# One modulation piece at a time between dense weight slabs, three bank turns, and moved operands in a two-block transformer kernel

## The chip, the cores and the metric

The kernel runs on one core of a Trainium2 chip, as one program. The metric is the device time of that program in microseconds. Before the change it is 2503.66 us, the median of three runs (2502.77 to 2505.79).

## The reference

Two blocks of two layers each, over 256 tokens of width 1024, all in float32. In short:

```python
def first_block(x, ...):
    for l in range(2):
        h = rms_norm(x, norm_mix_pre[l])
        u = h @ w_in[l]                              # 1024 x 6484
        ys = [mamba2(u), fox(u), moba(u), dsa(u)]    # four branches, 512 wide each
        gates = sigmoid(h @ w_gate[l] + b_gate[l])   # four times 1024
        mix = (sum of gates * (ys @ w_branch[l])) @ w_out[l]
        x = x + rms_norm(mix, norm_mix_post[l])
        h = rms_norm(x, norm_ffn_pre[l])
        g, up = split(h @ w_ffn_in[l], 2)            # 2816 each
        x = x + rms_norm((silu(g) * up) @ w_ffn_out[l], norm_ffn_post[l])

def second_block(x, ctx, c, c_ctx, ...):             # adaLN block on x and on ctx
    for l in range(2):
        # six modulations of width 1024 for the tokens and six for the context
        m = silu(cvec) @ w_mod_2[l] + b_mod_2[l]     # 1024 x 6144
        shift1, scale1, gate1, shift2, scale2, gate2 = split(m, 6)
        h = rms_norm(x) * (1 + scale1) + shift1
        p = h @ w_in_2[l]                            # 2560 columns
        # chunked linear mixing (256), differential attention (4 heads, 512),
        # and a gated convolution of 31 taps (256) side by side
        x = x + gate1 * (y @ w_out_2[l])
        h = rms_norm(x) * (1 + scale2) + shift2
        x = x + gate2 * ((act(h @ w_gate_2[l]) * (h @ w_val_2[l])) @ w_down_2[l])
```

The modulation does not depend on x, so it may be computed at any time before its use. Layer 0 of the second block works on the tokens and on the context (four tiles of 128 rows), layer 1 on the tokens alone (two tiles), and so does the whole first block.

## The kernel before

Every dense product streams its weights. A slab is two blocks of 128 rows by 512 columns (512 KB). SP loads it into one of four ring slots (`wraw`, L898). ScalarE rounds it to the matmul's short format (`whi`, L1009), VectorE makes the rest (`wlo`, L816), and PE multiplies three times for each block and tile: high by high, high by low, low by high (L1770). A slab of two tiles is 12 matmuls of 512 columns, one of four tiles 24. ScalarE and VectorE are three slabs ahead of PE (`AHEAD`). Eight PSUM banks hold the results; the dense products take them in turns of four, the attention and small steps take the other four.

One planner in Python writes a single list of steps, and each engine walks this list in order and does its part of each step. So what stands in the list before something stands before it on every engine. The steps are slabs of the dense products, with the work of the branches woven in between (`weave`, `interleave`).

The modulation product has its own path. Its slabs (`mod_slabs`, 4 slabs for 512 columns, 24 such chunks) aren't split; PE multiplies the raw weights in full precision with the two condition vectors, in four column groups of the array at once. ScalarE copies the sums (`modrow`, L1050), PE adds the groups up and turns them (`mod_cols`) or spreads them over the rows (`mod_gate`), and VectorE adds the bias. The chunks are put at places between two stages (`filler`, `fill`), in the second block's attention (the gates), and between chunks of the second FFN. A ring slot with a modulation slab is free when PE has used it, where that of a dense slab is free as soon as it is split:

```python
if st.s >= RING_W:
    was = slabs[st.s - RING_W]
    need(sp, [was.used if was.evac == "mod" else was.split])
```

In the first block's attention each head's steps are `attn_s` (scores by PE, maximum by VectorE, exponentials by ScalarE, L1228), `attn_t` (PE turns the weights, ScalarE copies them as `probT`, L1232) and `attn_v` (values). In the second block's a unit's steps are `att2_s` (scores, maximum L1465, exponentials L1117), `att2_m` (reciprocal and the difference of two maps, L1472 to L1476), `att2_t` (turn, `aT`, L1123) and `att2_v`. In the stage with gates and branches every third slab's low half is made by POOL. The projections of the second block go to `p`, even tiles by ScalarE, odd ones by VectorE (L1320).

Of the kernel before, what the change touches and what calls it, by code (L numbers as in the profile page):

```python
# [48 lines left out]
RING_W, RING_S, AHEAD = 4, 4, 3  # L49
SLAB_K = 2  # L50
# [8 lines left out]
class Step:  # L59


    def __init__(self, kind, n=None, gain=None, x=None, sums0=None, out0=None, used=None, src=None, col=None,
# [5 lines left out]
                 d=None):  # L68
# [7 lines left out]
        self.ssq0, self.t, self.k0, self.sq, self.n0, self.pool, self.split, self.d = ssq0, t, k0, sq, n0, pool, split, d  # L76


class Planner:
# [6 lines left out]
    def __init__(self):  # L86
        self.steps = []
        self.uses = [0] * 8
        self.count = {}
        self.gemm_banks = 0  # L90
        self.turns = (0, 1, 2, 3)
        self.slabs = []
        self.first_slab, self.x_start = {}, {}
        self.dense = []
        self.mod_chunks = []
# [6 lines left out]
    def misc(self):  # L102

        return self.bank(FREE_BANKS[self.tick("free_turn") % 4])
# [46 lines left out]
def gemm(pl, weight, layer, act, tiles, nk, col0, width, evac, row0=0, kt0=0, ready=(), turned=False, **more):  # L151
# [3 lines left out]
    for c, (a, w) in enumerate(widths(width)):  # L155
# [3 lines left out]
        for k in range(0, nk, SLAB_K):  # L159
# [15 lines left out]
            if evac != "mod":  # L175
                st.d = len(pl.dense)
                pl.dense.append(st)
            steps.append(st)
    return steps


MOD_COLS = (0, 1, 2, 3, 6, 7, 8, 9)
MOD_GATES = (4, 5, 10, 11)


def mod_slabs(pl, l, c):


    n = len(pl.mod_chunks)
    war = pl.mod_chunks[n - 2] if n >= 2 else []  # L190
    pl.mod_chunks.append([])
    return gemm(pl, "w_mod_2", l, "cond", 1, KD, c * NW, NW, "mod", ready=[("cond_silu", 1)], mc=n, war=war)


def mod_reader(pl, slabs, bank):

    st = slabs[-1]
    l, c = st.layer, st.col // NW
    steps = []
    if c in MOD_GATES:  # L200
        banks = [bank(), bank()]
        steps.append(Step(kind="mod_gate", l=l, c=c, mc=st.mc, gate=c // 6, j=c % 2, waits=drained(*st.banks), banks=banks))
    else:
        banks = [bank()]
        steps.append(Step(kind="mod_cols", l=l, c=c, mc=st.mc, waits=drained(*st.banks), banks=banks))
        if c in (3, 9):
            steps.append(Step(kind="mod_gain", l=l, i=c // 6, waits=drained(*banks)))
    pl.mod_chunks[st.mc] += [(f"psum_full{b}", k + 1) for b, k in banks]
    return steps


def plan_first(pl):

    filler = list(MOD_COLS)
    for l in range(DEPTH):
# [32 lines left out]
        if l:  # L248
            pl.steps += mod_reader(pl, mods, pl.misc)
# [9 lines left out]
        def branch_splits(n, waits):  # L259
# [8 lines left out]
               (36, Step(kind="decay_turn", **decay)), (37, cb)]  # L268
        ybanks = [pl.bank(6), pl.bank(7)]
# [13 lines left out]
        def attention(br, qcol, waits):  # L283
# [4 lines left out]
            for i in range(HEADS + 3):  # L288
                for kind, h in (("attn_s", i), ("attn_v", i - 3), ("attn_t", i - 2)):
                    if 0 <= h < HEADS:  # L290
                        q = base + h
                        steps.append(Step(kind=kind, l=l, br=br, h=h, q=q, vcol=qcol + 2 * BW + h * HD,
                                          bank=pl.bank(4 + q % 2 + (0 if kind == "attn_s" else 2)),
# [62 lines left out]
        for st in pl.slabs[first:-len(g)]:  # L356
            st.pool = st.s % 3 == 0
# [3 lines left out]
        if l == 0:  # L361
            pl.add("cond")
# [5 lines left out]
        mods = mod_slabs(pl, 0, filler.pop(0))  # L368
        pl.steps.append(mods[0])
        postnorm(2 * l, out)  # L370
        pl.steps += mods[1:]
# [3 lines left out]
        pl.steps += mod_reader(pl, mods, pl.misc)  # L375
# [18 lines left out]
        mods = mod_slabs(pl, 0, filler.pop(0))  # L394
        pl.steps += mods + waiting + mod_reader(pl, mods, pl.misc)
        out = gemm(pl, "w_ffn_out", l, "hid", 2, KF, 0, D, "mix", ready=split_ready(hidden))
        pl.steps += out
        if l < DEPTH - 1:
            mods = mod_slabs(pl, 0, filler.pop(0))
            pl.steps.append(mods[0])  # L400
            postnorm(2 * l + 1, out)
            pl.steps += mods[1:]
        else:
            postnorm(2 * l + 1, out)


def plan_second(pl):

    filler = [(0, MOD_COLS[-1])] + [(1, c) for c in MOD_COLS]
    for l in range(DEPTH):  # L410
# [3 lines left out]
        def fill():  # L414

            return mod_slabs(pl, *filler.pop(0)) if filler else []

        def norm(i, tiles, summed):

            mods = fill()  # L420
            pl.steps.extend(mods[:1])
# [4 lines left out]
            pl.steps.extend(mods[1:])  # L426
# [5 lines left out]
            if mods:  # L432
                pl.steps += mod_reader(pl, mods, pl.misc)
# [10 lines left out]

        gc = project(C_C, T, ready)
# [31 lines left out]
        pl.steps += weave(gc + gq + gk + ga + gv, others)  # L477

# [7 lines left out]
        for i in range(len(units) + 2):  # L486
            for kind, u in (("att2_m", i - 1), ("att2_t", i - 2), ("att2_s", i), ("att2_v", i - 2)):
# [23 lines left out]
        stream = []  # L511
        agate = Step(kind="agate", l=l, tiles=T, n=aln[0].n, banks=[pl.gemm_bank(), pl.gemm_bank()])
        stream.append(agate)
        late = None
        for i, c in enumerate(MOD_GATES):
            g = mod_slabs(pl, l, c)
            stream += g
            if late:
                stream += mod_reader(pl, late, pl.gemm_bank)
            late = g  # L520
            if i == 1:
                cback = Step(kind="cback", l=l, tiles=T, banks=[pl.gemm_bank() for i in range(T // 2)])
                cln = ln(C_C, 2, drained(*cback.banks))
                cout = Step(kind="csilu", l=l, tiles=T, n=cln[0].n)
                stream += [cback, cln[0]]
            if i == 2:
                stream += [cln[1], cout]
        stream += mod_reader(pl, late, pl.gemm_bank)
# [3 lines left out]
        mods = fill()  # L532
        pl.steps += mods
# [6 lines left out]
        if mods:  # L540
            pl.steps += mod_reader(pl, mods, pl.misc)
# [16 lines left out]
        late = None  # L558
        base = pl.now("hid_lo")
        pl.turns = tuple(range(8))  # L560
        for c, (a, w) in enumerate(widths(FFN)):
            n0 = pl.now("hid_lo")
            for weight, evac in (("w_gate_2", "ffg"), ("w_val_2", "ffv")):
                pl.steps += gemm(pl, weight, l, "act2", T, KD, a, w, evac, ready=ready, turned=True, n0=n0)
                ready = ()
            pl.tick("hid_lo", w // P)
            if late:
                pl.steps += mod_reader(pl, late, pl.misc)
            late = fill() if c in (0, 1, 2, 3) else None
            pl.steps += late or []  # L570
        late = fill()
        pl.steps += late
        if late:
            pl.steps += mod_reader(pl, late, pl.misc)
# [12 lines left out]
def build(nc, A, out, second=True):  # L587
    pl = Planner()
    plan_first(pl)
    if second:  # L590
        plan_second(pl)
    slabs, dense = pl.slabs, pl.dense
# [4 lines left out]
    with ExitStack() as ctx:  # L597
# [44 lines left out]
        stream = sb("stream", [P, 4])  # L642
        cond = sb("cond", [P, KD, 2])
        condm = sb("condm", [P, KD, 32])
        modrow = sb("modrow", [P, 2, NW // 2])
# [4 lines left out]
        modg = sb("modg", [P, DEPTH, 2, KD, 2])  # L650
        psum = ctx.enter_context(nc.psum_tensor("psum", [P, 8, 512], F32))
# [7 lines left out]
        gains = sb("gains", [P, 1, D], F32, one)  # L659
        act_h = sb("act_h", [P, KD, SEQ], F32R, one)  # L660
# [90 lines left out]
        rstd4 = sb("rstd4", [P, 4], F32, two)  # L751
# [4 lines left out]
        p = sb("p", [P, 4, IN_COLS], F32, two)  # L756
        kT = sb("kT", [P, B_HEADS, 4 * P], F32, two)
# [66 lines left out]
        def _(sp):  # L824
# [5 lines left out]
            def load_parameters():  # L830
                o = P
                for t, n, parts in ((tri, P, P), (ones, P, P), (cmask, 3 * P, P), (smask, 3 * P, P), (cossin, 128, P),
                                    (negsel, 16, 16), (cossin2, 128, P), (stream, 4, P)):
# [37 lines left out]
            for st in slabs:  # L871
# [21 lines left out]
                if st.s >= RING_W:  # L893
                    was = slabs[st.s - RING_W]
                    need(sp, [was.used if was.evac == "mod" else was.split])
                w = A[st.weight]
# [1196 lines left out]
```

## Time and profile before

| | |
|---|---|
| median of 3 runs | 2503.66 us (2502.77 to 2505.79) |
| the profiled execution's own time | 2500.43 us |
| its span, first to last instruction | 2498.8 us |
| mean granted clock of TensorE | 0.940 |
| PE busy | 2247.9 us, 90% |
| VectorE (DVE) busy | 1425.2 us, 57% |
| ScalarE (ACT) busy | 1044.5 us, 42% |
| GpSimd (POOL) busy | 303.8 us, 12% |
| read from memory | 346.19 MB, 139 GB/s over the span |

Busy time is a union over an engine's instructions. What is left of the span for PE is idle time; a wait is put down to the instruction that released it. A granted clock of 1.00 is full speed.

### The profile page before, as it was taken

What the parts mean: (1) busy time and instruction counts of PE and PEld (TensorE: products, weight loads), DVE (VectorE), ACT (ScalarE), POOL (GpSimd) and SP (SyncE); (2) the same over time, 40 slices, a digit from 0 to 9 for tenths busy, and PEclk for the clock granted to TensorE, in tenths of its full rate; (3) what the DMA queues carried; (4) which work ended last, traced back from release to release, by engine and by line L of the source; (5) the groups of instructions that cost most, each with busy time, mean ns of one, the idle gap of its engine ahead of it and who ended that gap; (6) DMA issues with size and microseconds to landing.
All of it is one profiled execution on the core that took longest, in us unless ns stands there. A gap on an engine that the chain in (4) does not pass through costs nothing. (4 is left out here: it accounts for less than half of the span.)

```text
span 2498.8 us, 29164 instructions
## 1 busy us (share of the span) xinstructions
PE 2247.9 (90%) x11116; PEld 1796.6 (72%) x11116; DVE 1425.2 (57%) x2187; ACT 1044.5 (42%) x1664; POOL 303.8 (12%) x310
## 2 busy tenths in 40 slices
PE   8999898898999998979997877889989898887999
PEld 6777676787777776768876664667767787656997
DVE  5665574454465647545445886554444325966774
ACT  4545554443444455534443434322222223543443
POOL 0017120000000532210000540000000000600000
PEclk9999999999999999989998988889999998987999
DMA  7644335565555433466564213423333435333554
GB/s 227 185 124 127 105 115 160 181 177 183 191 175 157 141 102 95 138 201 180 160 205 159 63 51 93 135 93 110 101 101 110 135 101 168 94 119 117 162 183 161
DMA packets 184121, 349.15 MB, mean 140 GB/s; under 512 B 11824, under 2 KB 23216, under 8 KB 183984
## 3 DMA queue, kind: packets, MB, share of 16 engines
q1 hardware_dynamic: 183984, 347.29, 44.4%
q8 instruction: 90, 1.47, 0.2%
q14 instruction: 47, 0.39, 0.0%
HBM read 346.19 MB, written 1.05 MB: 139 GB/s over the span
## 5 line engine op out<-in xcount | busy, mean ns | idle before, releaser
L816 DVE TENSOR_TENSOR wlo<-wraw,whi 128x1024 fp32r<-128x1024 f32 (+1 forms) x538 | 646.2, 1207 | 682.0 <-ACT whi L1009 678.7
L1009 ACT ACTIVATE whi<-wraw 128x1024 fp32r<-128x1024 f32 (+1 forms) x552 | 562.7, 1027 | 648.0 <-PE psum L1770 546.3
L1770 PE MATMUL psum<-whi,act_h 128*128 128x512 f32 (+2 forms) x1424 | 578.4, 406 | 31.8 <-DVE p L1320 22.1
L1770 PE MATMUL psum<-wlo,act_h 128*128 128x512 f32 (+2 forms) x1424 | 564.7, 397 | 0.0
L1770 PE MATMUL psum<-whi,act_l 128*128 128x512 f32 (+2 forms) x1424 | 563.8, 396 | 0.0
L1770 PEld LDWEIGHTS psum<-whi,act_h 128*128 128x128 f32 x1424 | 277.1, 195 | 105.6 <-DVE p L1320 24.7
L1770 PEld LDWEIGHTS psum<-whi,act_l 128*128 128x128 f32 x1424 | 275.7, 194 | 62.2
L1770 PEld LDWEIGHTS psum<-wlo,act_h 128*128 128x128 f32 x1424 | 276.6, 194 | 56.5
L1770 PE MATMUL psum<-act_h,whi 128*128 128x512 f32 (+1 forms) x704 | 244.0, 347 | 23.7 <-DVE wlo L816 19.8
L1770 PE MATMUL psum<-act_l,whi 128*128 128x512 f32 (+1 forms) x704 | 242.2, 344 | 0.0
L1770 PE MATMUL psum<-act_h,wlo 128*128 128x512 f32 (+1 forms) x704 | 242.2, 344 | 0.0
L1770 PE MATMUL psum<-whi,hid_h 128*128 128x512 f32 x440 | 174.9, 397 | 0.0
L1770 PE MATMUL psum<-wlo,hid_h 128*128 128x512 f32 x440 | 174.1, 396 | 0.0
L1770 PE MATMUL psum<-whi,hid_l 128*128 128x512 f32 x440 | 173.8, 395 | 0.0
L1770 PEld LDWEIGHTS psum<-act_h,whi 128*128 128x128 f32 x704 | 135.9, 193 | 43.0 <-DVE wlo L816 22.2
L1770 PEld LDWEIGHTS psum<-act_l,whi 128*128 128x128 f32 x704 | 136.0, 193 | 16.4
L1770 PEld LDWEIGHTS psum<-act_h,wlo 128*128 128x128 f32 x704 | 135.3, 192 | 16.7
L1770 PEld LDWEIGHTS psum<-whi,hid_h 128*128 128x128 f32 x440 | 84.0, 191 | 18.8 <-issue 0.2
L1770 PEld LDWEIGHTS psum<-whi,hid_l 128*128 128x128 f32 x440 | 83.7, 190 | 19.0
L1770 PEld LDWEIGHTS psum<-wlo,hid_h 128*128 128x128 f32 x440 | 83.8, 191 | 18.4
L1773 PE MATMUL psum<-ident,p 128*128 128x128 f32 x228 | 46.4, 375 | 51.5 <-DVE p L1384 25.4
L1228 ACT ACTIVATE logit<-logit,nmax 128x128 f32<-128x128 f32 x96 | 42.9, 448 | 96.6 <-DVE nmax L1696 95.9
(270 smaller groups left out, 2693.4 us busy)
## 6 DMA issues: line engine op xcount, KB each, us to landing
wraw<-in_w_in SPq DMA_DIRECT2D x136, 512.0 KB, 3.7
wraw<-in_w_gate SPq DMA_DIRECT2D x104, 512.0 KB, 3.7
wraw<-in_w_mod SPq DMA_DIRECT2D x96, 512.0 KB, 3.7
wraw<-in_w_ffn_in SPq DMA_DIRECT2D x80, 512.0 KB, 3.7
wraw<-in_w_ffn_out SPq DMA_DIRECT2D x44, 512.0 KB, 4.2
wraw<-in_w_down SPq DMA_DIRECT2D x44, 512.0 KB, 4.3
wraw<-in_w_val SPq DMA_DIRECT2D x40, 512.0 KB, 4.6
wraw<-in_w_branch SPq DMA_DIRECT2D x32, 512.0 KB, 3.9
```

Of the source, the lines that this page charges most:

```text
L816: eng.tensor_tensor(wlo[:, i, 0:st.n, 0:st.w], wraw[:, st.s % RING_W, 0:st.n, 0:st.w], whi[:, i, 0:st.n, 0:st.w].bitcast(F32), ALU.subtrac ...
L1009: nc.scalar.activation(whi[:, d % RING_S, 0:st.n, 0:st.w], wraw[:, s % RING_W, 0:st.n, 0:st.w], ACT.Copy).then_inc(sem("slab_rounded"), 1)
L1228: nc.scalar.activation(logit[:, i, a:b], logit[:, i, a:b], ACT.Exp, bias=nmax[:, r, t:t + 1], accum_out=rsum[:, r, t:t + 1]).then_inc(sem( ...
L1770: return nc.tensor.matmul(out, lhsT, rhs, start=start, stop=stop)
L1773: return nc.tensor.transpose(out, src, ident[:, :])
```

## The change

Seven edits in one.

1. The modulation weights come from the host as 96 pieces of 128 columns by all 1024 rows (`w_mod_pieces`, 512 KB in one contiguous run for each partition). A piece is one step, `mod_ride`, put behind a dense slab: every fifth in the first block (64 pieces), every second in the second block's projections and every fifth in its FFN (8 each, in both layers). The reader of a piece stands with the next piece. The fillers between stages and in the second attention are gone. Pieces and readers have a PSUM bank of their own.
2. The dense products of the first block take three banks in turn instead of four; those of the second FFN seven instead of eight.
3. ScalarE evacuates all tiles of `p`.
4. First block's attention: a new step `attn_e` holds the exponentials; the order is scores, turn with copy, exponentials, values.
5. Second block's attention: `att2_t`, `att2_s`, `att2_m`, `att2_v`, where it was m, t, s, v.
6. No low half is made by POOL.
7. Padding in SBUF: `act`, `y`, `hid`, `act2` (0 or 352 modulo 512 bytes before) start at 384 modulo 512, as `hid2` already did.

```diff
 RING_W, RING_S, AHEAD = 4, 4, 3
+OPERAND_AT, OPERAND_STEP = 384, 512
-        self.turns = (0, 1, 2, 3)
+        self.turns = (0, 1, 2)
+        self.free = FREE_BANKS
+        self.mod_queue, self.mod_every, self.mod_since, self.mod_bank = [], 5, -8, 3
...
+            pl.mod_since += 1
+            if pl.mod_queue and pl.mod_since >= pl.mod_every:
+                pl.mod_since = 0
+                st.after = mod_ride(pl)
...
+def mod_ride(pl):
+    l, c = pl.mod_queue.pop(0)
+    steps = mod_reader(pl)
+    n = len(pl.mod_reads)
+    st = Step(kind="slab", s=len(pl.slabs), weight="w_mod_2", layer=l, c=c, evac="mod", mc=n, banks=[pl.bank(pl.mod_bank)],
+              first=True, last=True, war=pl.mod_reads[n - 2] if n >= 2 else [])
+    b, use = st.banks[0]
+    st.used = (f"psum_full{b}", use + 1)
+    pl.slabs.append(st)
+    pl.mod_last = st
+    return steps + [st]
...
-                for kind, h in (("attn_s", i), ("attn_v", i - 3), ("attn_t", i - 2)):
+                for kind, h in (("attn_s", i), ("attn_t", i - 2), ("attn_e", i), ("attn_v", i - 3)):
...
-        for st in pl.slabs[first:-len(g)]:
-            st.pool = st.s % 3 == 0
...
-        mods = mod_slabs(pl, 0, filler.pop(0))
         ms = [split("scr", 256 * g, [("merged", pl.now("merged"))], "ym", 2 * g) for g in range(4)]
-        pl.steps += mods + ms + mod_reader(pl, mods, pl.misc)
+        pl.steps += ms
...
+    pl.free, pl.mod_bank, pl.turns = (4, 5, 6), 7, (0, 1, 2, 3)
...
+        pl.mod_queue, pl.mod_every, pl.mod_since = [(l, c) for c in MOD_GATES[0]], 2, -4
...
-            for kind, u in (("att2_m", i - 1), ("att2_t", i - 2), ("att2_s", i), ("att2_v", i - 2)):
+            for kind, u in (("att2_t", i - 2), ("att2_s", i), ("att2_m", i - 1), ("att2_v", i - 2)):
...
+        pl.mod_queue, pl.mod_every, pl.mod_since = [(l, c) for c in MOD_GATES[1]], 5, 0
-        pl.turns = tuple(range(8))
+        pl.turns = tuple(range(7))
...
+        at_offset("pad_one", one)
         act_h = sb("act_h", [P, KD, SEQ], F32R, one)
...
-                        for t in range(0, st.tiles, 2):
+                        for t in range(st.tiles):
                             filled(act, st.banks[t])
...
-                    for k in range(st.n):
-                        for i in range(2):
-                            r = 32 * (2 * k + i)
-                            ins = dot(psum[r:r + 32, bk[0], 0:half], condm[:, st.kt + k, :],
-                                      wraw[:, st.s % RING_W, k, i * half:(i + 1) * half], st.first, st.last)
+                    for k in range(KD):
+                        r = 32 * (k % 4)
+                        ins = dot(psum[r:r + 32, bk[0], 0:P], condm[:, k, :], w[:, k * P:(k + 1) * P], k < 4, k >= 4)
```

PE at the border from w_branch to w_out in layer 0 of the first block, before. `y_h` and `y_l` are the halves of a branch's output or of the merged one, `x` in the turning row is the merged output.

```order
L1770 MATMUL psum<-wlo,y_h 128x512
L1770 MATMUL psum<-whi,y_l 128x512
L1770 MATMUL psum<-wraw,condm 32x256 x16
L1773 MATMUL psum<-ident,x 128x128 x16
L1770 MATMUL psum<-stream,modrow 128x2 x4
L1770 MATMUL psum<-whi,y_h 128x512
```

The same engine and place after.

```order
L1748 MATMUL psum<-wlo,y_h 128x512
L1748 MATMUL psum<-whi,y_l 128x512
L1751 MATMUL psum<-ident,x 128x128 x16
L1748 MATMUL psum<-whi,y_h 128x512
L1748 MATMUL psum<-wlo,y_h 128x512
```

The four modulation slabs (16 products with `condm`) and their reader have left; only the turning stands between the two dense products.

PE inside w_in of layer 0, after, between two dense slabs, where nothing but dense rows stood before.

```order
L1748 MATMUL psum<-whi,act_l 128x512
L1748 MATMUL psum<-stream,modrow 128x2
L1748 MATMUL psum<-wraw,condm 32x128 x8
L1748 MATMUL psum<-whi,act_h 128x512
L1748 MATMUL psum<-wlo,act_h 128x512
```

The reader of the piece before and a new piece of 8 products have come in here, with 128 columns instead of 256.

VectorE in the second block's attention, before; one unit's round.

```order
L1480 TENSOR_SCALAR p<-psum,ri 128x128
L1472 RECIPROCAL ri<-rs 128x2
L1474 TENSOR_SCALAR ri<-ri,rs,lam 128x1
L1476 SCALAR_TENSOR_TENSOR e<-e,ri 128x512
L1465 TENSOR_REDUCE nm<-psum 128x1 x2
L1467 TENSOR_SCALAR nm<-nm 128x2
```

The same after.

```order
L1443 TENSOR_REDUCE nm<-psum 128x1 x2
L1445 TENSOR_SCALAR nm<-nm 128x2
L1450 RECIPROCAL ri<-rs 128x2
L1452 TENSOR_SCALAR ri<-ri,rs,lam 128x1
L1454 SCALAR_TENSOR_TENSOR e<-e,ri 128x512
L1458 TENSOR_SCALAR p<-psum,ri 128x128
```

The rows are the same; the values' scaling, which stood between a unit's maximum and its own reciprocal, now stands behind the mix, and the reciprocal behind the maximum is the previous unit's.

## Rows read from the trace of the kernel before

**Rows 1.** First part of the page: busy us (share of the span), count, each engine.
```profile
PE 2247.9 (90%) x11116; PEld 1796.6 (72%) x11116; DVE 1425.2 (57%) x2187; ACT 1044.5 (42%) x1664; POOL 303.8 (12%) x310
```

**Rows 2.** PE's waits by releaser: us in total, times, longest us.
```profile
PE psum L1770 <- ACT aT L1123: 25.5, 12, 6.3
...
PE psum L1770 <- DVE p L1320: 22.4, 7, 8.8
PE psum L1770 <- ACT probT L1232: 21.3, 17, 2.9
```

**Rows 3.** Windows, PE alone (us, PE busy, PEclk, DMA, GB/s): 20, 6, 20, 20 slabs.
```profile
603.22:659.22 56.00, 56.00 (x241) 1.00 0.54 171
1664.51:1698.11 33.60, 33.60 (x145) 1.00 0.27 79
1968.14:2076.94 108.80, 108.80 (x482) 1.00 0.27 87
2435.50:2489.90 54.40, 54.40 (x242) 1.00 0.51 169
```

**Rows 4.** Windows of all engines: two of 17 border stretches, and the sum.
```profile
408.95:421.47 12.52, 5.60 (x57) 4.39 (x57) 6.76 (x8) 6.33 (x9) 2.03 (x2) 0.86 0.73 245
...
2082.47:2101.54 19.07, 11.47 (x74) 8.80 (x73) 15.95 (x27) 8.07 (x14) 1.40 (x3) 0.62 0.81 282
sum 209.10, PE 97.12 PEld 72.84 DVE 135.91 ACT 102.09 POOL 13.81; mean PE 5.71 PEld 4.28 DVE 7.99 ACT 6.01 POOL 0.81
```

**Rows 5.** Timeline of the border to w_out (start, us, engine, ..., idle before).
```profile
408.95 1.93 PE L1770 MATMUL psum<-wraw,condm 128*32 128x256 f32 x32
...
409.65 9.77 SPq L898 DMA_DIRECT2D wraw<-in_w_out  x7
...
411.16 1.97 PE L1773 MATMUL psum<-ident,x 128*128 128x128 f32 x16 [0.27 <-POOL x L932]
414.00 1.06 ACT L1009 ACTIVATE whi<-wraw 128x1024 fp32r<-128x1024 f32 x1 [12.10 <-DMA wraw<-in_w_out]
...
419.77 1.84 PE L1770 MATMUL psum<-stream,modrow 128*128 128x2 f32 x8 [6.65 <-DVE y_l L1578]
```

**Rows 6.** Windows: a first slab behind a border, and a layer 1 border without filler.
```profile
598.70:603.22 4.52, 4.52 (x13) 3.58 (x14) 1.30 (x2) 0.00 (x0) 0.00 (x0) 0.60 0.88 304
...
2261.07:2267.06 5.99, 2.62 (x18) 2.42 (x16) 4.14 (x15) 2.48 (x12) 1.20 (x2) 0.80 0.21 80
```

**Rows 7.** Windows: the second block's attention, layers 0 and 1.
```profile
1491.38:1575.66 84.28, 62.57 (x386) 36.36 (x384) 58.25 (x158) 37.16 (x120) 4.80 (x8) 0.84 0.33 100
2201.40:2261.07 59.67, 47.35 (x302) 28.23 (x301) 38.75 (x87) 26.94 (x68) 2.36 (x4) 0.83 0.49 160
```

**Rows 8.** Timeline of PE in the first block's attention.
```profile
291.07 0.92 PE L1770 MATMUL psum<-U,probT 128*128 128x64 f32 x6 [2.92 <-ACT probT L1232]
```

**Rows 9.** Groups by line and shape: busy us, mean ns, idle before, releasers.
```profile
L816 DVE TENSOR_TENSOR wlo<-wraw,whi 128x1024 fp32r<-128x1024 f32 x498 | 617.6, 1246 | 647.0 <-ACT whi L1009 643.8
...
L1770 PE MATMUL psum<-wraw,condm 128*32 128x256 f32 x768 | 58.5, 430 | 3.1 <-DVE modT L1362 3.1
...
L816 POOL TENSOR_TENSOR wlo<-wraw,whi 128x1024 fp32r<-128x1024 f32 x14 | 33.5, 2390 | 197.6 <-ACT whi L1009 197.6
L1770 PE MATMUL psum<-stream,modrow 128*128 128x2 f32 x128 | 25.8, 323 | 47.8 <-ACT modrow L1050 20.1 <-DVE y_l L1578 13.1 <-DVE act_l L1583 12.7
...
L1320 DVE COPY p<-psum 128x512 f32<-128x512 f32 x17 | 11.3, 684 | 8.7 <-PE psum L1770 8.7
L1371 DVE TENSOR_TENSOR gates<-gates,psum 128x512 f32<-128x512 f32 x16 | 10.8, 686 | 5.5 <-PE psum L1770 4.9
```

**Rows 10.** Window: the second block's projections in layer 0.
```profile
1345.00:1491.00 146.00, 126.53 (x519) 101.42 (x519) 111.11 (x132) 61.12 (x89) 65.86 (x49) 0.90 0.23 71
```

More of the change, by code:

```diff
@@ L174, in gemm @@
             pl.slabs.append(st)
-            if evac != "mod":
-                st.d = len(pl.dense)
-                pl.dense.append(st)
+            st.d = len(pl.dense)
+            pl.dense.append(st)
             steps.append(st)
-    return steps
[L182 to L192, printed above, removed]
@@ L195, in mod_reader @@
[L195 to L208, printed above, removed]
+            pl.mod_since += 1
@@ new lines, in mod_reader @@
+def mod_reader(pl):
+    st, pl.mod_last = pl.mod_last, None
+    if st is None:
+        return []
+    l, c, part = st.layer, st.c, st.c // KD
+    bk = pl.bank(pl.mod_bank)
+    pl.mod_reads.append([(f"psum_full{bk[0]}", bk[1] + 1)])
+    if part in (2, 5):
+        return [Step(kind="mod_gate", l=l, c=c, mc=st.mc, gate=part // 3, j=c % KD, waits=drained(*st.banks), banks=[bk])]
+    steps = [Step(kind="mod_cols", l=l, c=c, mc=st.mc, waits=drained(*st.banks), banks=[bk])]
+    if part in (1, 4) and c % KD == KD - 1:
+        steps.append(Step(kind="mod_gain", l=l, i=part // 3, waits=drained(bk)))
@@ L209, in mod_reader @@
     return steps
 def plan_first(pl):
-    filler = list(MOD_COLS)
+    pl.mod_queue = [(i, c) for i in range(DEPTH) for c in MOD_COLS]
     for l in range(DEPTH):
@@ L393, in plan_first @@
             hidden += waiting
-        mods = mod_slabs(pl, 0, filler.pop(0))
-        pl.steps += mods + waiting + mod_reader(pl, mods, pl.misc)
+        pl.steps += waiting
         out = gemm(pl, "w_ffn_out", l, "hid", 2, KF, 0, D, "mix", ready=split_ready(hidden))
         pl.steps += out
[L398 to L404, printed above, removed]
+        postnorm(2 * l + 1, out)
 def plan_second(pl):
-    filler = [(0, MOD_COLS[-1])] + [(1, c) for c in MOD_COLS]
+    assert not pl.mod_queue
+    pl.steps += mod_reader(pl)
+    pl.free, pl.mod_bank, pl.turns = (4, 5, 6), 7, (0, 1, 2, 3)
     for l in range(DEPTH):
@@ L509, in plan_second @@
         att += pending
-        stream = []
         agate = Step(kind="agate", l=l, tiles=T, n=aln[0].n, banks=[pl.gemm_bank(), pl.gemm_bank()])
[L513 to L528, printed above, removed]
+        cback = Step(kind="cback", l=l, tiles=T, banks=[pl.gemm_bank() for i in range(T // 2)])
+        cln = ln(C_C, 2, drained(*cback.banks))
+        stream = [agate, cback, cln[0], cln[1], Step(kind="csilu", l=l, tiles=T, n=cln[0].n)]
         pl.steps += interleave(stream, att)
         pl.turns = (0, 1, 2, 3)
-        mods = fill()
-        pl.steps += mods
         order = [0, 1, 6, 7, 2, 3, 4, 5]
@@ L566, in plan_second @@
             pl.tick("hid_lo", w // P)
[L567 to L574, printed above, removed]
+        assert not pl.mod_queue
+        pl.steps += mod_reader(pl)
         pl.turns = (0, 1, 2, 3)
@@ L591, in build @@
         plan_second(pl)
+    pl.steps = [one for st in pl.steps for one in [st] + st.after]
     slabs, dense = pl.slabs, pl.dense
@@ L1316, in _ @@
                                                      ).then_inc(free(st.banks[t]), 1)
-                    if st.evac == "p":
-                        for t in range(1, st.tiles, 2):
-                            filled(dve, st.banks[t])
-                            dve.tensor_copy(p[:, t, st.col:st.col + st.w], psum[:, st.banks[t][0], 0:st.w]
-                                            ).then_inc(free(st.banks[t]), 1)
                     if st.evac == "res":
@@ L2041, in constants @@
     cs2 = np.stack([np.cos(ang2), np.sin(ang2)], 1).reshape(2, P, 64).transpose(1, 0, 2).reshape(P, 128)
-    rows = np.zeros((P, 4))
-    for half in range(2):
-        for s in range(2):
-            rows[[32 * half + s, 64 + 32 * half + s], 2 * half + s] = 1
+    rows = np.zeros((P, 2))
+    for j in range(4):
+        rows[[32 * j, 32 * j + 1], [0, 1]] = 1
     return np.concatenate([eye, upto, np.ones((P, P)), later, zero, later, later.T, zero, later.T, cs, neg, cs2, rows],
```

101 lines of the change are left out of this document (49 added, 52 removed).

## The prediction, written before the changed kernel was run

> **What bounds the kernel now.** I read the page's first part, the waits of PE by releaser, tables of windows, and then the timeline around single waits. PE is busy for 2247.9 of 2498.8 us [rows 1], so the time is PE's work plus the stretches in which it stands. The waits [rows 2] are few and long, and none belongs to the steady stream of weights: they lie in the attention stages and at the borders between stages. In the steady stream a slab of two tiles (12 matmuls) takes 2.80 us and one of four tiles 5.60 (56.00/20 and 33.60/6); only w_down, whose operand is hid2, runs at 2.72 and 5.44 (54.40/20, 108.80/20), all at the full granted clock [rows 3]. Seventeen stretches hold the modulation slabs that stand at borders: together 209.10 us, with PE busy in 97.12 [rows 4].
>
> **Borders: −118 and −13.** The border from w_branch to w_out shows the mechanism [rows 5]. SP issues w_out's first weights at 409.65, after PE has used the first modulation slab, since the ring of four frees a slot only then. They land at 414.00, 4.35 us later, ScalarE copies three in a row, the split of y waits behind them, and PE, done with the four transposes of y at 413.1 (411.16 + 1.97), stands 6.65 us, until 419.77. With no modulation slab there, the dense weights are prepared before the border, and only transposes, split and first slab remain. My estimates after: 4.2 us at each of the two w_branch→w_out borders (the wait for the merge, four transposes of 0.5 us, the last split), 6.4 at each of three norm borders in the first block, 1.1 before each w_ffn_out, 20.3 at the entry of the second block, 9.7 at the first ysplit, 15.8 at each of two four-tile norms (now 19.07: its chain of DVE work, 15.95 us busy, stays), nothing at the six places in the second FFN: 8.4 + 19.2 + 2.2 + 20.3 + 9.7 + 31.6 = 91.4, so −118. A border of layer 1 that carries no filler today takes 5.99 us [rows 6], which speaks for 6.4. The slab behind a border costs extra: the first of w_ffn_out takes 4.52 us at a granted clock of 0.60 where 2.80 is normal [rows 6]. Where PE no longer stands, its clock stays up and this goes: eight places × 1.6 us = −13. Bounds: −100 (the chains of vector work are late everywhere) to −145.
>
> **Second block's attention: −28.** The two stages take 84.28 and 59.67 us with PE busy in 62.57 and 47.35, DVE in 58.25 and 38.75 [rows 7]. A unit is a loop: DVE's max, ScalarE's exponentials, DVE's reciprocal and mix, PE's transpose, aT; PE waits 25.5 us on aT in all [rows 2]. The new order lets DVE do the next unit's max ahead of this unit's mix, so that the exponentials lie beside DVE's work. 28 units in 143.95 us are 5.1 us each, ramps and side work included. I count 0.4 us for each of the 28 from the order, 11. Besides, 16 gate adds of 0.69 leave DVE (11 us, L1371 [rows 9]), and a third of the modulation slabs and the readers of gates leave PE; in a loop that waits on both engines in turn I count 17 for the two. Bounds −10 to −40.
>
> **First block's attention: −10.** One head's turned weights (probT, on ScalarE) stand behind the next head's exponentials and often behind a weight copy of 1.06 us: PE waits 21.3 us on probT [rows 2], 2.92 of them in one piece [rows 8]. With the copy ahead of the exponentials I take half of the 21.3 off, since the weight copy can still stand ahead of it. Against it, 14 low halves leave POOL, which took 2.39 us for each, for DVE, 14 × 1.25 = 17.5 us [rows 9]; nobody waits there on POOL, and DVE has room in most of these stages, so +3. Bounds 0 to −20, and 0 to +10.
>
> **Evacuations of p: −2.** 17 DVE copies of 0.68 us leave [rows 9]; PE waited 22.4 us behind them. In the projections DVE is busy for 111.11 of 146 us [rows 10] and has no gap in the part with rotations, so that nine copies (−6) leave and eight gate adds (+3.4) and the landing of pieces come; ScalarE takes all four tiles in a row instead of two. Bounds −12 to +8.
>
> **Where the operands lie: −42.** act, y, hid, act2 are moved to the offset that hid2 has now. Nothing else separates the 226.7 from the 232.5 ns per matmul that rows 3 show: the same lines, shapes, clock and evacuations; the weights lie where they lie in both. Rotations and ring traffic speak neither way. If every slab takes hid2's pace: 332 two-tile slabs of the first block × 0.08 = 26, in the second about 60 four-tile ones × 0.16 = 10, and 6 for the rest: −42. Bounds 0 and −50. The Trainium skill ("SBUF — State Buffer", "Who interferes with whom") says that "PE and ACT never wait on anyone" there. By it an address would cost nothing and the term is 0. The rows show two paces that no neighbour's traffic explains, so I follow the trace; no row shows act at the new place.
>
> **Rides: +73.** 96 pieces of 8 matmuls with 128 columns and their readers stand between dense slabs. The trace shows each of these products as two matmuls. A slab of before is 8 of them with 256 columns, and four slabs took 1.93 us [rows 5], 0.48 each; a piece is 16 with 128 columns, as many columns, and I take 0.46. A reader of before was 8 matmuls in 1.84 us at a low clock [rows 5] and 25.8/128 = 0.20 each over all [rows 9]; now it is 2, for which I take 0.22 at the full clock; a gate's reader has 4 and gets 0.45. Change-over 0.1. 64 × 0.8 + 32 × 1.0 = 83, of which 10 lies beside DVE-bound projections: +73. What this work costs now lies in the windows and stages already counted, and is not taken off again. Bounds +45 to +90.
>
> **Landing behind each piece: +53.** This is the new wait. A piece's slot in the ring is freed by PE's use. The dense slab four places on is therefore issued only then and needs 4.0 to 4.4 us to land [rows 5]. ScalarE walks in order and stands at that copy; copy and low half are done 6.4 us after the piece, and PE wants the slab after three slabs, 8.2 us: no wait for weights. But every evacuation behind the copy comes late, and the first block has now three bank turns instead of four. A chunk whose last slab is the first or second behind a piece frees its banks 1 to 2.8 us too late. By the plan that is 16 rides with the last slab directly behind and 15 one further on, of the two-tile kind: 16 × 1.9 + 15 × 0.8 = 43; attention stages, where ScalarE's exponentials stand behind the landing too, another 10. Three banks without any piece: +5. Bounds 10 and 80.
>
> **Sum.** −131 − 28 − 10 + 3 − 2 − 42 + 73 + 53 + 5 = −79 against the profiled execution's 2500.43, so 2421; that run is 3.2 below the median of the timed runs, 2503.66, and I add that: 2424.6, say **2424**. It is one sum of big terms of both signs, uncertain to ±35.
>
> **Rivals.**
> Addresses are nothing. For: the skill's rule, and that a tile's pace could hang on something I don't see, such as evacuation. Against: rows 3. It gives 2424 + 42 = 2466.
> The landing hides. For: in four-tile slabs there is twice the time, and many evacuations have slack; ScalarE is 42% busy [rows 1]. Against: three turns. It gives 2424 − 53 = 2371.
> Slower than before: ScalarE, in order behind a landing, starves the prefetch. If copy and low half are done later than 8.2 us after the piece, each ride costs PE's wait in full, and the next piece comes before the lead of three slabs is rebuilt. For: piece and slabs are 512 KB alike, and a landing at a border took 4.35 us. Against: 1.8 us of slack. It decides from 9.3 us on: 1.1 us more for each of some 75 two-tile rides is 83, which gives 2507.
> That the borders don't shorten since DVE's chains set them: −100 instead of −131 and no extras, 2455.
>
> **Chances.** My sum 0.45 (2385 to 2450), addresses nothing 0.20, landing hidden 0.20, borders kept by DVE 0.11, starved 0.04. The range 2378 to 2468 takes in most of each neighbour. A difference of 0.2%, 5 us, is about what a measurement of this kernel tells from none; only the last rival and a tail of the others reach it: faster 0.95, within 0.02, slower 0.03.
>
> **What the profile after would show.** Slabs of two tiles at 2.72 us in w_in and w_ffn_out, of four at 5.44 in w_gate_2 (else the address term is gone). The waits of PE on modrow, y_l and act_l nearly absent, and no stretch over 2 us before w_ffn_out. ScalarE waiting about 4 us for the weights once per piece, and PE waiting 1 to 3 us for an evacuation after some of them; if these add to under 15 us, the second rival is right. The second attention's stages near 70 and 46 us. I am wrong at the root if PE waits on low halves behind most pieces, or if the border windows keep 9 us and more.

## The result and the profile after

The changed kernel takes 2635.26 us (median of 4 runs, 2628.35 to 2642.45) against 2504.72 for the kernel before in the same comparison: a ratio of 1.052, 95% interval 1.0489 to 1.0551. The prediction was 2424, a gain of 79; the result is a loss of 131.

The first part of the page after: PE stands more and is busy longer, VectorE and ScalarE do what they did in [rows 1].

```profile
span 2640.8 us, 31204 instructions
PE 2278.4 (86%) x11948; PEld 1853.8 (70%) x11948; DVE 1430.2 (54%) x2248; ACT 1067.7 (40%) x1751; POOL 261.9 (10%) x296
```

PE's waits by releaser after, in the form of [rows 2].

```profile
PE psum L1748 <- DVE modT L1341: 75.5, 63, 7.6
PE psum L1748 <- DVE gates L1348: 73.7, 28, 10.6
PE psum L1751 <- DVE p L1362: 32.6, 4, 11.3
PE psum L1751 <- DVE e L1454: 29.5, 18, 3.6
PE psum L1748 <- ACT aT L1107: 14.9, 11, 5.0
...
PE psum L1748 <- ACT probT L1216: 3.4, 4, 1.0
```

Two rows stand above all others and are new: 149.2 us in 91 waits, on VectorE's reading of the modulation sums. There are 96 pieces, so nearly each has its wait. The group row of the pieces' matmuls says that it is they who wait (the ones of before stood 3.1 us, [rows 9]).

```profile
L1748 PE MATMUL psum<-wraw,condm 128*32 128x128 f32 x1536 | 67.0, 294 | 149.3 <-DVE modT L1341 75.5 <-DVE gates L1348 73.7
```

One ride in the timeline (first block, layer 0) shows the chain.

```profile
258.06 0.28 PE L1748 MATMUL psum<-stream,modrow 128*128 128x2 f32 x2
...
258.60 1.99 ACT L992 ACTIVATE whi<-wraw 128x1024 fp32r<-128x1024 f32 x2
259.67 1.23 DVE L795 TENSOR_TENSOR wlo<-wraw,whi 128x1024 fp32r<-128x1024 f32 x1 [3.87 <-ACT whi L992]
260.81 0.21 DVE L1341 TENSOR_SCALAR modT<-psum,cols 128x2 f32<-128x2 f32 x1
...
261.17 0.95 PE L1748 MATMUL psum<-wraw,condm 128*32 128x128 f32 x16 [2.83 <-DVE modT L1341]
```

PE does the reader of the last piece at 258.06 into bank 3. The next thing on PE is the new piece, and it writes bank 3 too. So it must wait until VectorE has read the reader's two columns. That read takes 0.21 us, but VectorE walks in order and has a low half ahead of it, which waits for ScalarE's rounding. PE stands 2.83 us for a read of 0.21.

The second new thing is the wait that the prediction did name. ScalarE's waits on weight landings are 355 us in 178 waits, where the kernel before had 112 in 51. A case behind a ride in w_out, from the timeline:

```profile
491.79 1.95 SPq L881 DMA_DIRECT2D wraw<-in_w_out  x2
...
495.55 1.06 ACT L992 ACTIVATE whi<-wraw 128x1024 fp32r<-128x1024 f32 x1 [3.47 <-DMA wraw<-in_w_out]
...
496.64 1.23 DVE L795 TENSOR_TENSOR wlo<-wraw,whi 128x1024 fp32r<-128x1024 f32 x1 [4.56 <-ACT whi L992]
497.79 1.28 DVE L1291 TENSOR_TENSOR x<-psum,gains 128x512 f32<-128x512 f32 x2
...
498.52 0.50 PE L1748 MATMUL psum<-whi,y_h 128*128 128x512 f32 x1 [2.47 <-DVE x L1291]
```

The slab that takes the piece's slot is sent for at 491.79, after PE has used the piece; ScalarE and then VectorE stand for it; VectorE's evacuation of a finished chunk comes 1.2 us behind the low half, and PE, with three banks, waits 2.47 us for it.

The operands' pace is as predicted: ten two-tile slabs of w_in at the full clock.

```profile
22.50:49.70 27.20, 27.20 (x122) 1.00 0.66 202
```

The borders have shrunk, though not all to my figures (here w_out to w_ffn_in with reader and piece in it, then the last part of the way from w_ffn_in to w_ffn_out, then the four-tile norm ahead of layer 1 of the second block), and the second block's attention takes 74.20 and 43.60 us. That doesn't compare with the 84.28 and 59.67 of [rows 7] as they stand: those windows open 1.8 and 1.6 us earlier, at the products with `wsT`, and the ones below at the first scores (`kT,qT`).

```profile
508.19:515.61 7.42, 3.64 (x36) 3.08 (x34) 6.42 (x12) 3.95 (x10) 1.09 (x3) 0.89 0.47 161
667.00:669.79 2.79, 0.38 (x4) 0.41 (x5) 2.24 (x4) 0.26 (x1) 0.00 (x0) 1.00 0.73 247
...
2175.00:2192.90 17.90, 8.00 (x39) 6.54 (x38) 13.57 (x24) 5.63 (x13) 1.40 (x3) 0.71 0.59 205
1644.50:1718.70 74.20, 46.84 (x217) 28.65 (x217) 51.75 (x148) 35.75 (x115) 5.16 (x8) 0.79 0.07 23
2317.40:2361.00 43.60, 26.45 (x134) 16.71 (x134) 28.67 (x74) 20.04 (x54) 2.08 (x4) 0.88 0.14 46
```

The kernel before, from the first scores on:

```profile
1493.20:1575.66 82.46, 60.75 (x378) 35.03 (x377) 56.80 (x156) 36.45 (x119) 4.80 (x8) 0.83 0.34 103
2203.00:2261.07 58.07, 46.09 (x294) 27.29 (x294) 37.54 (x84) 26.23 (x67) 2.36 (x4) 0.82 0.51 164
```

So the two stages fell by 8.3 and 14.5 us.

### The profile page after: what moved, and what is told of

The parts are those of the page before. It is cut to its first block and busy times, and to the rows that moved or that the text cites. A ratio compares the mean times of both kernels' runs of the same rounds, so it can differ in the third digit from the quotient of the medians.

```text
span 2640.8 us, 31204 instructions
## 1 busy us (share of the span) xinstructions
PE 2278.4 (86%) x11948; PEld 1853.8 (70%) x11948; DVE 1430.2 (54%) x2248; ACT 1067.7 (40%) x1751; POOL 261.9 (10%) x296
## 5 line engine op out<-in xcount | busy, mean ns | idle before, releaser
L795 DVE TENSOR_TENSOR wlo<-wraw,whi 128x1024 fp32r<-128x1024 f32 (+1 forms) x552 | 660.6, 1203 | 757.5 <-ACT whi L992 753.8
L1748 PE MATMUL psum<-whi,act_h 128*128 128x512 f32 (+2 forms) x1424 | 585.4, 411 | 25.8 <-DVE work L1298 8.1
L1748 PE MATMUL psum<-wlo,act_h 128*128 128x512 f32 (+2 forms) x1424 | 564.8, 397 | 0.0
L1748 PE MATMUL psum<-whi,act_l 128*128 128x512 f32 (+2 forms) x1424 | 564.3, 396 | 0.0
L1748 PEld LDWEIGHTS psum<-whi,act_h 128*128 128x128 f32 x1424 | 281.9, 198 | 101.7 <-issue 16.3
L1748 PEld LDWEIGHTS psum<-whi,act_l 128*128 128x128 f32 x1424 | 279.4, 196 | 58.4
L1748 PEld LDWEIGHTS psum<-wlo,act_h 128*128 128x128 f32 x1424 | 281.5, 198 | 51.0
L1748 PE MATMUL psum<-act_h,whi 128*128 128x512 f32 (+1 forms) x704 | 245.1, 348 | 11.6 <-DVE ft L1324 5.3
L1748 PE MATMUL psum<-act_l,whi 128*128 128x512 f32 (+1 forms) x704 | 242.2, 344 | 0.0
L1748 PE MATMUL psum<-act_h,wlo 128*128 128x512 f32 (+1 forms) x704 | 241.9, 344 | 0.0
L1748 PE MATMUL psum<-wraw,condm 128*32 128x128 f32 x1536 | 67.0, 294 | 149.3 <-DVE modT L1341 75.5
L1748 PE MATMUL psum<-whi,hid_h 128*128 128x512 f32 x440 | 173.7, 395 | 0.9 <-DVE tmp L1291 0.9
L1748 PE MATMUL psum<-whi,hid_l 128*128 128x512 f32 x440 | 172.5, 392 | 0.0
L1748 PE MATMUL psum<-wlo,hid_h 128*128 128x512 f32 x440 | 172.4, 392 | 0.0
L1748 PEld LDWEIGHTS psum<-act_h,whi 128*128 128x128 f32 x704 | 138.5, 197 | 30.6 <-DVE ft L1324 5.7
L1748 PEld LDWEIGHTS psum<-wraw,condm 128*32 128x32 f32 x1536 | 41.6, 114 | 158.9 <-issue 158.8
L1748 PEld LDWEIGHTS psum<-act_h,wlo 128*128 128x128 f32 x704 | 138.4, 197 | 14.4
L1748 PEld LDWEIGHTS psum<-act_l,whi 128*128 128x128 f32 x704 | 138.6, 197 | 13.9
L1033 ACT ACTIVATE modrow<-psum 128x128 f32<-128x128 f32 x96 | 26.5, 276 | 231.5 <-PE psum L1748 231.5
L1748 PEld LDWEIGHTS psum<-whi,hid_h 128*128 128x128 f32 x440 | 83.6, 190 | 19.3 <-DVE tmp L1291 1.3
L1748 PEld LDWEIGHTS psum<-whi,hid_l 128*128 128x128 f32 x440 | 83.3, 189 | 17.6
```

Source lines behind the costliest of these rows:

```text
L795: eng.tensor_tensor(wlo[:, i, 0:st.n, 0:st.w], wraw[:, st.s % RING_W, 0:st.n, 0:st.w], whi[:, i, 0:st.n, 0:st.w].bitcast(F32), ALU.subtrac ...
L1033: nc.scalar.activation(modrow[:, st.mc % 2, :], psum[:, st.banks[0][0], 0:P], ACT.Copy).then_inc(free(st.banks[0]), 1)
L1748: return nc.tensor.matmul(out, lhsT, rhs, start=start, stop=stop)
```

## The experiments

Ratios are against the kernel before on the same chip.

**x1_reader_early.** The reader stands two dense slabs ahead of the next piece, in the projections one.

```diff
                 st.after = mod_ride(pl)
+            elif pl.mod_last and pl.mod_since == max(1, pl.mod_every - 2):
+                st.after = mod_reader(pl)
```

> The changed kernel with one edit: a piece's reader stands two dense slabs ahead of the next piece (in the projections one) instead of directly before it; all else as changed, the shared bank too. Theory A (reader and next piece use one PSUM bank, so PE stands at the piece until DVE, in order behind its other work, has read the reader's sums): PE's waits on modT (75.5 us) and gates (73.7 us) nearly vanish and the time falls by 110 to 150, to about 2500. Theory B (ScalarE and DVE are late since they stand behind the landing of the slab that reuses a piece's ring slot, and A's waits are only where this shows): the waits move to other releasers and the time falls by less than 40, to 2595 or more.

2523.93 us, ratio 1.0073 (1.0040 to 1.0105): 111 us less than the changed kernel by medians (0.0447 by the ratios, 112 us). PE's waits on modT are gone, those on gates are 13.5 us in 5.

```profile
L1750 PE MATMUL psum<-wraw,condm 128*32 128x128 f32 x1536 | 63.2, 283 | 13.6 <-DVE gates L1350 13.5
```

Theory A holds, at the lower end of its band of 110 to 150, and the bank waits are not merely where lateness from landing shows: ScalarE still waits 312 us for landings here. The group's waits fell by 136 us and the time by 111, so some 25 came back elsewhere: PE's waits on ybuf, for one, grew from 8.9 to 18.6 us, those on low halves from 2.5 to 13.8.

**x2_own_slot.** Pieces land in a tile of their own, and the dense ring counts dense slabs only.

```diff
+        mraw = sb("mraw", [P, D])
...
-                    need(sp, [was.used if was.evac == "mod" else was.split])
...
+                if st.evac == "mod":
+                    if st.mc:
+                        need(sp, [pieces[st.mc - 1].used])
+                    sp.dma_start(mraw[:, :], A["w_mod_pieces"][st.layer, st.c]).then_inc(sem("piece_landed"), 16)
+                    continue
+                if st.d >= RING_W:
+                    need(sp, [dense[st.d - RING_W].split])
```

> The changed kernel with one edit: pieces land in a 4 KB slot of their own, so that the dense ring never waits for a piece's use; all else as changed. Theory B: ScalarE's waits on weight landings (some 320 us) vanish, and with them most of PE's, the time falls by 90 or more, to 2545 or less. Theory A: the waits of PE on modT and gates stay above 100 us and the time falls by 30 to 60 only, the landing term of the prediction.

2561.17 us, ratio 1.0214 (1.0175 to 1.0254): 74 less than the changed kernel. ScalarE's waits on landings fall from 355 to 61 us, PE's waits of the pieces stay whole:

```profile
L1751 PE MATMUL psum<-mraw,condm 128*32 128x128 f32 x1536 | 68.2, 298 | 152.0 <-DVE gates L1351 79.7 <-DVE modT L1344 72.3
```

So the landing is a real cost of 74 us, outside what either theory gave it (30 to 60, or 90 and more), and it is not the cause of the bank waits.

**x3_both.** Both edits.

> Both edits together: early reader and own slot. If A and B are two independent losses the gains add, and the time is near 2450, within 30 of what the prediction had without landing plus the bank wait (2371 is its figure for a hidden landing). If one is the cause of the other, both together give little more than the better one alone.

2457.94 us, ratio 0.9798 (0.9764 to 0.9833). Against the changed kernel −177, where the single edits sum to −185: two nearly independent losses. This kernel is 2.0% below the one before (1.7 to 2.4%). The longest waits left on PE are those of the stages themselves; of the bank waits 12.3 us on gates are left, in 4 waits, all in the two projection stages.

```profile
PE psum L1756 <- DVE p L1367: 32.7, 4, 11.4
PE psum L1756 <- DVE e L1459: 26.2, 18, 3.6
PE psum L1756 <- DVE ybuf L1687: 17.0, 15, 2.9
PE psum L1753 <- ACT aT L1112: 14.9, 11, 5.0
```

**x4_no_pad.** The changed kernel without padding.

```diff
-        at_offset("pad_common", ctx)
...
-        at_offset("pad_one", one)
```

> The changed kernel without the padding: act, y at 0 and hid, act2, hid2 at 352 modulo 512 as before. Theory address: two-tile slabs go back from 2.72 to 2.79 us everywhere, w_down's included, and the time rises by 35 to 50, to about 2677. Theory clock or neighbours: no change.

2664.17 us, ratio 1.0615 (1.0575 to 1.0654): 29 us slower than the changed kernel by medians, 24 by the ratios, less than the 35 to 50 expected. Ten two-tile slabs of w_in take 28.00 us where the changed kernel takes 27.20:

```profile
22.05:50.05 28.00, 28.00 (x122) 1.00 0.66 199
```

The sharpest test is w_down. Its operand hid2 lay at 384 in the kernel before and lies at 352 here, with the same line, shape and clock. Ten four-tile slabs, first here, then in the kernel before:

```profile
2101.07:2157.07 56.00, 56.00 (x242) 1.00 0.29 94
```

```profile
1989.90:2044.30 54.40, 54.40 (x242) 1.00 0.29 97
```

The pace follows the address, and not the product.

**b1_pad.** The kernel before with the padding alone (the same lines, put into it, and `rstd4` behind `p`, where the changed kernel has it).

> The kernel before with the padding alone: act, y, hid, act2 at 384 modulo 512, as hid2. Theory address: two-tile slabs 2.72 us instead of 2.79, four-tile ones 5.44 instead of 5.60, and the time falls by 30 to 45 (the prediction's term is 42; taking the padding out of the changed kernel cost 29). Rival: a faster stream is given back at waits for DVE and ScalarE, fall under 15.

2481.04 us, ratio 0.9906 (0.9886 to 0.9926): 24 us less (19 to 29), outside both bands. Dense stretches run at 2.72 us in its trace too, but not every stage keeps the whole gain: the w_ffn_out stages fall by 1.6 and 1.9 us, which is 22 slabs at 0.08, the w_ffn_in stages, with 44 slabs, by 2.0 and 2.5 only, and the second FFN of layer 0 by 3.6 where 44 four-tile slabs at 0.16 would give 7.

**b2_three_turns.** The kernel before with three turns in the first block.

```diff
-        self.turns = (0, 1, 2, 3)
+        self.turns = (0, 1, 2)
...
+    pl.turns = (0, 1, 2, 3)
```

> The kernel before with three bank turns instead of four in the first block (bank 3 idle), nothing else. The prediction's term is 5 us. Rival: the turns are the reason for what the mixer stages lose, 15 or more.

2512.60 us, ratio 1.0031 (1.0015 to 1.0047): 8 us (4 to 12). The turns alone are a small cost.

**x5_pool.** x3 with every third low half of the stage with gates and branches on POOL.

```diff
+        for st in pl.slabs[first:last]:
+            st.pool = st.evac != "mod" and st.s % 3 == 0
```

> The kernel with early reader and own slot, and every third low half of the stage with gates and branches made by POOL again, as before the change. Theory: DVE is late in that stage since it makes all low halves; the stage of layer 0 (262 us against 241 before the change) falls by 8 or more. Rival: POOL's 2.4 us per half are no better, change within 3 us.

2453.10 us, ratio 0.9799 (0.9775 to 0.9823), against 0.9798 for x3: no difference that these runs can tell. The stage of layer 0 took 257 us in this trace against 262 in x3's, that of layer 1 241 against 246. Neither theory is borne out: x9 below has x3's stage unchanged, without POOL's halves, and took 256 and 241, so five us lie within what this stage varies by from trace to trace.

**x6_old_attention.** x3 with the first block's old order.

```diff
-                for kind, h in (("attn_s", i), ("attn_t", i - 2), ("attn_e", i), ("attn_v", i - 3)):
+                for kind, h in (("attn_s", i), ("attn_e", i), ("attn_v", i - 3), ("attn_t", i - 2)):
```

> The kernel with early reader and own slot, and the order of the first block's attention as before the change (scores with exponentials, values, turn with copy). The prediction says that the new order is worth 10 us: this one is slower by 5 to 15. Rival: in the new order the exponentials come later and DVE's last sums (ybuf) with them, so that this one is faster by 5 to 15; PE's waits on ybuf (17.0 us) then fall.

2455.83 us, ratio 0.9806 (0.9784 to 0.9828): the same as x3, so neither the 5 to 15 slower nor the 5 to 15 faster. The waits changed places. Here they are with the old order; with the new one ybuf has 17.0 and ScalarE's probT 4.3 us.

```profile
PE psum L1753 <- ACT probT L1221: 23.3, 14, 4.5
...
PE psum L1756 <- DVE ybuf L1687: 1.2, 2, 0.7
```

**x7_p_dve.** x3 with the odd tiles of p evacuated by VectorE.

```diff
-                        for t in range(st.tiles):
+                        for t in range(0, st.tiles, 2):
...
+                    if st.evac == "p":
+                        for t in range(1, st.tiles, 2):
+                            filled(dve, st.banks[t])
+                            dve.tensor_copy(p[:, t, st.col:st.col + st.w], psum[:, st.banks[t][0], 0:st.w]
+                                            ).then_inc(free(st.banks[t]), 1)
```

> The kernel with early reader and own slot, and the odd tiles of p evacuated by VectorE again. The prediction says that the move to ScalarE is worth 2 us. In this kernel the projections take 159 and 111 us against 149 and 102 before the change. Theory: the 16 gate rides cost that, the evacuation is neutral, change within 4 us. Rival: ScalarE's four evacuations in a row hold its weight copies and cost 8 or more, so that this kernel is faster by 8 or more and the two projection stages fall by 4 each.

2457.24 us, ratio 0.9814 (0.9790 to 0.9838). The two projection stages take 161.4 and 112.4 us in its trace, 159.1 and 111.0 in x3's, so they hint at up to 4 us for the move to ScalarE; the time shows nothing. The prediction's 2 is neither shown nor refuted.

**x8_pool_p_dve.** x5 and x7 together.

> The kernel with early reader and own slot, with VectorE's share of p and POOL's share of the low halves both restored: what is left of the change is rides, moved operands and the two attention orders. Expected from the single runs, if they add: 2448 to 2458.

2462.66 us, ratio 0.9828 (0.9800 to 0.9857). A little above the band, and within the intervals of x3; neither of the two edits decides anything.

**b3_att2_order.** The kernel before with the second attention's new order alone.

```diff
-            for kind, u in (("att2_m", i - 1), ("att2_t", i - 2), ("att2_s", i), ("att2_v", i - 2)):
+            for kind, u in (("att2_t", i - 2), ("att2_s", i), ("att2_m", i - 1), ("att2_v", i - 2)):
```

> The kernel before with the second block's attention in the new order alone (turn, scores, mix, values), its modulation slabs left in place. The prediction gives the order 11 us of its 28. Theory: the two stages fall from 84 and 58 us by 4 to 8 each and the time by 8 to 16. Rival: the order is nothing by itself, all of the gain comes from the modulation work that leaves the stage, fall under 4.

2496.33 us, ratio 0.9968 (0.9950 to 0.9986): 8 us (4 to 13), at the lower edge of the 8 to 16 expected. Windows of its two attention stages, from the first scores to the end of the stage:

```profile
1505.42:1585.17 79.75, 58.51 (x377) 33.95 (x376) 56.35 (x156) 37.22 (x119) 4.88 (x8) 0.87 0.36 106
2211.91:2263.86 51.95, 42.16 (x294) 24.35 (x294) 37.15 (x84) 25.07 (x66) 2.36 (x4) 0.90 0.59 180
```

Against 82.46 and 58.07 before they fell by 2.7 and 6.1. PE's waits on aT fell from 25.5 to 5.7 us, and most of that came back as waits on VectorE's mix (`e`, L1476), 7.1 before and 24.5 here.

**x9_no_gate_rides.** x3 without the 16 rides in the two projection stages. It leaves work out: the first gate of both layers of the second block is its bias alone.

```diff
-        pl.mod_queue, pl.mod_every, pl.mod_since = [(l, c) for c in MOD_GATES[0]], 2, -4
+        pl.mod_queue, pl.mod_every, pl.mod_since = [], 2, -4
```

> The kernel with early reader and own slot, without the 16 rides of the two projection stages: the first gate of both layers of the second block is its bias alone. The prediction books these rides at 1.0 us each and hides 10 of the 16 beside VectorE, so 6 us. Theory: VectorE has no room there, each ride's gate add and the bank's and slot's waits are late, and the stages fall by 8 to 14 each, the time by 18 to 28. Rival: as the prediction has it, fall under 10; what these stages lose is then from elsewhere.

2432.21 us, ratio 0.9699 (0.9678 to 0.9720), which is 25 us below x3 for 16 rides, 1.6 each. The windows of the two stages, first of x3, then of this kernel:

```profile
1362.30:1521.40 159.10, 134.71 (x690) 108.82 (x688) 114.04 (x136) 72.37 (x110) 65.22 (x49) 0.89 0.26 87
...
2056.60:2167.60 111.00, 98.91 (x534) 78.75 (x532) 81.27 (x128) 58.11 (x98) 39.80 (x45) 0.92 0.37 124
```

```profile
1348.20:1492.60 144.40, 121.50 (x532) 99.77 (x530) 113.46 (x128) 69.84 (x102) 65.76 (x49) 0.91 0.24 70
2028.70:2130.20 101.50, 87.06 (x374) 71.26 (x372) 82.66 (x120) 56.14 (x90) 40.04 (x45) 0.89 0.34 104
```

They fall by 14.7 and 9.5. VectorE's busy time hardly moves (114.04 to 113.46, 81.27 to 82.66), PE's falls by 13.2 and 11.9, some 1.6 for a ride. PE is the busier engine in both stages (134.71 us of 159.10, VectorE 114.04), so work given to PE has little room to hide there. PE's 12.3 us of bank waits go too, but its longest wait on VectorE's `p` in the first stage grows from 10.5 to 17.9 us. That wait ends 125.9 us after the stage's start, where it ended after 134.4 with the rides, so they also delay VectorE; what in them does so is not settled.

## Why the prediction was wrong

**The failing step: rides, +73.** The prediction priced a ride as PE work: piece 0.46, reader 0.22 or 0.45, change-over 0.1. It named the bank that pieces and readers have to themselves in the description of the change and never asked who must empty it between the reader and the piece directly behind it. That wait was in no term and in none of the rivals. It cost 111 us: x1 takes it away by moving the reader, with the bank still shared. The reader does the same work in its new place, so it is the distance between two fills of one bank that decides. (No run gave the readers a bank of their own.) The work as such was sized fairly where nothing else binds: in x3's trace, from start to the next start, a piece takes 0.57, a column reader 0.14 and a gate's reader 0.36 us. But of the 16 gate rides ten us were said to lie beside VectorE's work, so that 6 were left, and x9 shows 25.

**Landing, +53: right in kind, 74 in size.** x2 shows 74 with the bank waits present, and x3 against x1 66. It lies within the bounds of 10 and 80. The rival in which it hides is refuted, and the one in which ScalarE's prefetch starves too: PE waits on low halves for 2.5 us in all after the change, 3 times, and in x1, without the bank waits, for 13.8 us in 9, where that rival needs 83. The time is past its 2507, but not by its mechanism.

**Borders, −118 and −13: nearly right.** Measured from the last dense slab's nominal end to the first of the next, in x3's trace w_branch→w_out takes 5.3 us twice (4.2 said), the norms 7.4, 6.8 and 7.4 (6.4), w_ffn_out 1.2 and 2.4 (1.1), the entry 21.0 (20.3), the first ysplit 10.4 (9.7), the four-tile norms 17.0 each (15.8): 101 us where the sum had 91.4. The second FFN of layer 0 falls from 304 to 252 us. In the changed kernel itself the first is 11.2 in layer 0, since the last merge stands behind a landing.

**Operands, −42: right in kind, 24 in size.** The rule that "PE and ACT never wait on anyone" (the Trainium skill, "SBUF — State Buffer", "Who interferes with whom") gives 0; b1_pad gives 24 (19 to 29), x4 24 by the ratios and 29 by medians, with nothing changed but addresses. (The prediction's 232.5 ns is a slip: 56.00/240 and 33.60/144 are 233.3. Its 0.08 and 0.16 us for a slab are right.) The trace disagrees with the rule as I applied it. The step that failed in size is "if every slab takes hid2's pace": each one with 512 columns does, but in b1 the second FFN of layer 0 kept 3.6 us of some 7, and the products of 256 columns in layer 1's second FFN got slower (last section), so that this stage took 1.7 longer.

**Second attention, −28: 23.** The two stages fell by 8.3 and 14.5 us, 23 together; of these the order alone is 8 (b3), where I said 11. The wait on aT went as said, but most of it came back as a wait on VectorE's mix.

**First attention, −10: wrong.** The wait on probT fell from 21.3 to 3.4 us, by more than the half that was said, and came back as a wait on VectorE's ybuf (x6 against x3). The split off POOL, +3, cannot be told from nothing (x5). **p, −2:** cannot be told from nothing either (x7). **Three turns, +5:** 8.

By the measured sizes: from 2424, the bank's 111, landing 21 more, operands 18 less gained, gate rides 19 more, borders 10, first attention 10, second attention 5 and turns 3 more make 2621. That is bookkeeping, since the sizes come from different kernels and need not add. The other 14 us to 2635 aren't settled by a run. Candidates that the traces show: the slab behind a stand is slow, with the granted clock down. Nine times, twelve dense matmuls (as many as a two-tile slab has) came right behind a piece that had stood 3.4 to 7.6 us for its bank; they took 3.8 to 5.3 us instead of 2.72, the first of them like this (PE alone, after; 0.65 is the granted clock):

```profile
77.50:81.70 4.20, 4.20 (x16) 0.65 0.73 229
```

The stage with gates and branches takes 262 and 246 us in x3 against 241 and 240, 27 us more, of which the own work of its 20 rides, at 0.7, is 14; and the second FFN of layer 1 takes 140 against 128, with 8 pieces in it. But the stage with gates and branches varied by itself: in b3, whose first block is that of before, it took 250.5 us in layer 0.

## What to carry to other kernels

When steps share a PSUM bank, write down for each pair of fills in a row who reads between them and what that engine has ahead of the read in its own order; a read of 0.2 us can cost PE 3 if it stands behind other work. Put the fill that reads a result a few steps away from the next use of its bank. A ring that holds two kinds of data, one freed at preparation and one at use, makes all its users wait for the slower kind; a slot apart was worth 74 us here for 4 KB per partition.

## What was not expected of the hardware

The start address of the activations, with the same shapes and the full clock, changes the pace of a stream of matmuls of 512 columns: 28.00 us for ten slabs of w_in with `act` at 0 modulo 512 bytes, 27.20 at 384 (233.3 against 226.7 ns each), and the same two paces for w_down with `hid2` at 352 and at 384 (x4). In these products the moved tile is the stationary operand (L1748's weight loads are `psum<-whi,act_h 128x128`) and the 512 columns that stream through are those of `whi` and `wlo`, which did not move. In w_gate_2 and w_val_2 the activations are the moving operand, and there four-tile slabs show the same step, 5.60 to 5.44 us (x4 against after). With two tiles these products have 256 columns, and the step goes the other way. Ten slabs of 24 such matmuls in the second FFN of layer 1, in the kernel before and in b1 (118.3 and 120.0 ns each):

```profile
2310.89:2339.28 28.39, 28.39 (x242) 1.00 0.55 170
```

```profile
2286.66:2315.45 28.79, 28.79 (x243) 1.00 0.55 164
```

Why 384 is the faster place for one shape and the slower for the other no run shows, and no other offset was tried.

Pieces land later than slabs of the same 512 KB in the kernel after: 5.7 us in the median against 4.1 to 4.6 for the dense weights.

```profile
wraw<-in_w_in SPq DMA_DIRECT2D x136, 512.0 KB, 4.4
wraw<-in_w_gate SPq DMA_DIRECT2D x104, 512.0 KB, 4.1
wraw<-in_w_mod_pieces SPq DMA_DIRECT2D x96, 512.0 KB, 5.7
```

It is not their layout. In x2 and x3, where a piece has a slot of its own, the same pieces land in 3.7 us, and the modulation slabs of before took 3.7 as well. The line of x2:

```profile
mraw<-in_w_mod_pieces SPq DMA_DIRECT2D x96, 512.0 KB, 3.7
```
